# Mix stage of a two-block transformer kernel: three of the four out-projection pieces get their low parts on GpSimd, and the convolution's square is placed ahead of the last copies

## The chip, the cores and the metric

The kernel runs on one core of one Trainium2 chip. The metric is the device time of one execution in microseconds (us). Three timed runs of the kernel before gave 1586.13, 1586.66 and 1586.75 us; the median is 1586.66 us.

## What is computed

The input is 256 tokens of width 1024, in fp32. A first block runs two layers of feed-forward, mixer and feed-forward. A second block, where the change lies, is

```python
hn = rms_norm(h, attn_norm_g[l])
proj = jnp.einsum('bsd,de->bse', hn, w_in[l])
xc, b_gate, c_gate, q, k, v = jnp.split(proj, split_points, axis=-1)
y_conv = short_conv_group(xc, b_gate, c_gate, conv_w[l], conv_out_g[l])
y_attn = diff_attention_group(q, k, v, ...)
mix = jnp.concatenate([y_conv, y_attn], axis=-1)
h = h + jnp.einsum('bse,ed->bsd', mix, w_out[l])
hn2 = rms_norm(h, ffn_norm_g[l]).reshape(Bsz * S, D)
y_ffn = hierarchical_moe(hn2, ...)      # 4 x 8 experts, top 2
```

The first half of `mix` (512 columns) is `b_gate` times a causal convolution of width 3 over `c_gate * xc`, normed in 8 groups; the second half is a four-head differential attention. The 32 experts' weights, 6 MB each, are all read from HBM.

## The kernel before

**Pieces.** Every weight matrix outside the experts goes through a ring of three slots in pieces of 128x2048 fp32. SP's queue loads a piece into `raw`; ACT (ScalarE) rounds it into `high` (`round_piece`, the operation on L249); DVE (VectorE) subtracts, `low = raw - high` (`split_piece`, L253); TensorE multiplies with three products per term (`product`, L258 to L260). The semaphore `split` counts finished subtractions over the whole program, `rounded` the roundings, and `used` the pieces that TensorE is done with. A slot is loaded again (`piece_loads`, L243) when the piece three before it is split, and rounded into when that piece is used.

**The mix stage.** Pieces 0 to 11 are the in-projection, six chunks of 512 columns, each in two pieces; pieces 12 to 15 are the out-projection. Each engine has its own order of work, written out by hand (`mix_pe`, `mix_act`, `mix_dve`, `mix_conv_pool`), and the engines meet at semaphores. The chunks are copied out of PSUM by ACT (`copies(n)`, L1722 for the first 128 tokens and L1725 for the second); `copies(5)` is the value chunk, without which the attention's outputs (`outs`, L1684 to L1687) can't begin. `outs(tt)` waits for the copy of its tokens.

**The convolution.** DVE forms `u` (L1938). GpSimd then issues seven DMAs that write `u`, moved down by one and by two rows, into `shifted` (L1992, L1997). DVE multiplies the unmoved part (`conv_unshifted`, L1886), then splits piece 12, then runs `conv()`: L1891 and L1892 on the moved parts, two sums (L1893, L1894) and the gate (L1897), which raises `m["conv"]`. Each of these reads two tensors in SBUF, as do L1903 and L1911 in `conv_norm()`. ACT squares the result (L1766), DVE sums the squares by group (L1905), ACT takes the root (L1768), DVE inverts it (L1908) and scales (L1911). That raises `h_ready`, for which TensorE waits before it transposes the convolution's half (`turn_half(tt, 0)`, L1673). ACT rounds the transposed half (L1772), DVE subtracts (`low_half`, L1915), and the products of pieces 12 and 13 begin. Pieces 14 and 15 belong to the attention's half and follow.

**Fillers.** `hold_clock(n)` (L1695) issues n products of the identity matrix whose result is not read; in the records each gives two matmuls.

**Behind the stage.** The out-projection is followed by the norm, the router and the expert stage. Its first loads wait on `h_ready`, `split` and `used` (`moe_sp`, L2255 in `load`); from the second batch on, each load waits until TensorE is done with the slot's last contents.

Of the kernel before, what the change touches and what calls it, by code (L numbers as in the profile page):

```python
# [95 lines left out]
def build(nc, t, out):  # L96
    ctx = ExitStack()
    with ctx:
# [65 lines left out]
        def banks(a, n=1):  # L164
            return psum[:, a:a + n, :].rearrange("p b n -> p (b n)")
# [674 lines left out]
        def columns(name, n):  # L840

            c = {"gla_in": (0, 1, 4, 2, 3, 5), "mix_in": (3, 4, 0, 2, 1, 5)}.get(name, range(IN_CHUNKS))[n]
            return slice(c * BANK, (c + 1) * BANK)
# [761 lines left out]
        def both(off, n):  # L1605
            return proj[:, :, off:off + n]
# [9 lines left out]
        def mix_pe(pe):  # L1616
            done = IN_DONE["mix_in"]

            def turn_qk(i):

                pe.wait_ge(m["qk"], i + 1)
                turn_columns(pe, banks(3 + 2 * i, 2), QK + i * D_CONV, DA_HEADS, m["qkT"])

            def dots(hd):

                pe.wait_ge(m["qk_sb"], 2)
                if hd >= 2:
                    pe.wait_ge(m["exp"], hd - 1)
                at = hd * TOKENS
                for c in range(2):  # L1630
                    rows, dst = slice(DA_HD * c, DA_HD * (c + 1)), banks(dot_banks(hd) + c)
                    pe.matmul(dst[:, 0:P], mqT[rows, at:at + P], mkT[rows, at:at + P], start=True, stop=False,
                              skip_group_check=True)
                for c in range(2):
                    rows, dst = slice(DA_HD * c, DA_HD * (c + 1)), banks(dot_banks(hd) + c)
                    ins = pe.matmul(dst[:, P:HEAD], mqT[rows, at + P:at + TOKENS], mkT[rows, at:at + TOKENS],
                                    start=False, stop=True, skip_group_check=True)
                    ins.then_inc(m["dots"], 1)

            def turn_a(hd):  # L1640
                pe.wait_ge(m["a"], hd + 1)
                if hd:
                    pe.wait_ge(m["aT_sb"], hd)
                for j in range(3):
                    ins = pe.transpose(TURN_X[:, j * P:(j + 1) * P], ma[hd % 2][:, j * P:(j + 1) * P], ident[:, :])
                ins.then_inc(m["aT"], 1)

            def after(n, r):
                at = 4 * n + r
                if at == 6:  # L1650
                    turn_qk(0)
                elif at == 10:
                    turn_qk(1)
                elif at == 12:
                    dots(0)
                elif at == 13:
                    dots(1)
                elif at == 15:
                    turn_a(0)
                    dots(2)  # L1660
                elif at == 16:
                    turn_a(1)
                    dots(3)
                elif at == 19:
                    turn_a(2)
                elif at == 20:
                    turn_a(3)

            def turn_half(tt, j):

                dst = banks((ATTN_BANK if j else CONV_BANK)[tt])
                for i in range(4):
                    ins = pe.transpose(dst[:, i * P:(i + 1) * P], h[:, tt, (4 * j + i) * P:(4 * j + i + 1) * P], ident[:, :])  # L1673
                ins.then_inc(turned, 1)

            def outs(tt):
                pe.wait_ge(in_copied[tt], done + IN_CHUNKS)
                pe.wait_ge(m["aT_sb"], DA_HEADS)
                dst = banks(ATTN_BANK[tt])
                for hd in range(DA_HEADS):  # L1680
                    a, col = maT[hd], slice(hd * DA_V, (hd + 1) * DA_V)
                    v0, v1 = (proj[:, i, VV + hd * DA_V:VV + (hd + 1) * DA_V] for i in range(TT))
                    if tt == 0:
                        ins = pe.matmul(dst[:, col], a[:, 0:P], v0, start=hd == 0, stop=True, skip_group_check=True)  # L1684
                    else:
                        pe.matmul(dst[:, col], a[:, P:2 * P], v0, start=hd == 0, stop=False, skip_group_check=True)
                        ins = pe.matmul(dst[:, col], a[:, 2 * P:], v1, start=False, stop=True, skip_group_check=True)  # L1687
                ins.then_inc(m["out"], 1)

            in_quarters(pe, "mix_in", 7, after)  # L1690

            def hold_clock(times):

                for _ in range(times):
                    pe.matmul(banks(3)[:, 0:P], ident[:, :], ident[:, :], start=True, stop=True, skip_group_check=True)  # L1695

            def front(products):
                outs(0)
                outs(1)
                hold_clock(9)  # L1700
                pe.wait_ge(h_ready, H_AT["mix"] + 1)
                for tt in range(TT):
                    turn_half(tt, 0)
                hold_clock(5)
                pe.wait_ge(turn_low, 4 * MIX_TURN + 1)
                products(0, 0)
                pe.wait_ge(turn_low, 4 * MIX_TURN + 2)
                products(0, 1)
                products(1, 0)
                for tt in range(TT):  # L1710
                    pe.wait_ge(h_ready, H_AT["mix"] + 2 + tt)
                    turn_half(tt, 1)
                products(1, 1)
                pe.wait_ge(turn_low, 4 * MIX_TURN + 4)
            out_pe(pe, "mix_out", 8, front)

        def mix_act(act, step):
            b, done = FIRST_PIECE["mix_in"], IN_DONE["mix_in"]

            def copies(n):  # L1720
                act.wait_ge(in_first, done + n + 1)
                act.activation(proj[:, 0, columns("mix_in", n)], banks((2 * n) % 3), ACT.Copy,  # L1722
                               scale=rstd[:, 0:1]).then_inc(in_copied[0], 1)
                act.wait_ge(used, b + 2 * n + 2)
                act.activation(proj[:, 1, columns("mix_in", n)], banks((2 * n + 1) % 3), ACT.Copy,  # L1725
                               scale=rstd[:, 1:2]).then_inc(in_copied[1], 1)

            def qk_root(i):

# [31 lines left out]
            def piece(i):  # L1761
                round_piece(act, b + i)

            def conv_root_act():
                act.wait_ge(m["conv"], 1)
                act.activation(both(XC, D_CONV), both(CG, D_CONV), ACT.Square).then_inc(m["sq"], 1)  # L1766
                act.wait_ge(m["sum"], 3)
                act.activation(conv_root, conv_sum, ACT.Sqrt, scale=8.0 / D_CONV, bias=eps[:, :]).then_inc(m["root"], 1)  # L1768

# [33 lines left out]
            turned_a(2)  # L1803
            turned_a(3)
            piece(13)
            copies(5)
            conv_root_act()
            act.wait_ge(used, b + IN_PIECES)
            for tt in range(TT):
                high_half(tt, 0, tt + 1)  # L1810
# [11 lines left out]
        def mix_dve(dve, step):  # L1822
            b, done = FIRST_PIECE["mix_in"], IN_DONE["mix_in"]

            def piece(i):
                split_piece(dve, b + i)
# [86 lines left out]
            def low_half(tt, j, number):  # L1913
                dve.wait_ge(turn_high, 4 * MIX_TURN + number)
                dve.tensor_tensor(turn_bank(hT_low, tt, j), banks((ATTN_BANK if j else CONV_BANK)[tt]).rearrange(  # L1915
                    "p (k n) -> p k n", n=P), turn_bank(hT_high, tt, j).bitcast(F32), ALU.subtract).then_inc(turn_low, 1)
# [25 lines left out]
            weights(3)  # L1942
            piece(11)
            conv_unshifted()
            piece(12)
            conv()
            conv_norm()
            dve.wait_ge(used, b + IN_PIECES)
            for tt in range(TT):
                low_half(tt, 0, tt + 1)  # L1950
            piece(13)
            for tt in range(TT):
                dve.wait_ge(m["sq"], tt + 4)
                dve.tensor_reduce(out_stat(tt, "sum"),
# [7 lines left out]
                                                   banks(ATTN_BANK[tt])[:, c], out_stat(tt, "inverse")[:, hd:hd + 1], sub_gain,  # L1962
                                                   ALU.mult, ALU.mult)
                ins.then_inc(h_ready, 1)
            piece(14)
            for tt in range(TT):
                low_half(tt, 1, tt + 3)
            out_dve(dve, "mix_out", 8)

        def mix_pool(pool, step):  # L1970
# [14 lines left out]
        def mix_conv_pool(pool, step):  # L1985

            pool.wait_ge(m["u"], 1)
            for rows in (slice(0, EVEN_ROWS), slice(EVEN_ROWS, P)):
                for i in range(2):
                    n = i + 1  # L1990
                    stop = min(rows.stop, P - n)
                    pool.dma_start(by_tile(shifted[i])[rows.start + n:stop + n, :, :],  # L1992
                                   both(XC, D_CONV)[rows.start:stop, :, :]).then_inc(m["shifted"], 16)
            for i in range(2):
                n = i + 1
                for r in range(n):
                    pool.dma_start(shifted[i][r:r + 1, D_CONV:2 * D_CONV],  # L1997
                                   proj[P - n + r:P - n + r + 1, 0, XC:XC + D_CONV]).then_inc(m["shifted"], 16)


        pa = route_tables[:, :]
# [737 lines left out]
```

## Time and profile before

| | us |
|---|---|
| median of the timed runs | 1586.66 |
| profiled execution | 1583.56 |
| its span, first to last instruction | 1581.8 |
| TensorE busy | 1454.2 (92%) |
| VectorE busy | 855.5 (54%) |
| ScalarE busy | 604.5 (38%) |
| GpSimd busy | 33.1 (2%) |

The profile is of one execution; its times are counted from the span's start. The mix stage's in-projection ends at about 1076 us, its out-projection at about 1107 us, and the expert stage fills the rest. Busy shares are averages over stages with different limits, so what follows reads single stages.

### The profile page before, as it was taken

What the parts mean: (1) busy time and instruction counts of PE and PEld (TensorE: products, weight loads), DVE (VectorE), ACT (ScalarE), POOL (GpSimd) and SP (SyncE); (2) the same over time, 40 slices, a digit from 0 to 9 for tenths busy, and PEclk for the clock granted to TensorE, in tenths of its full rate; (3) what the DMA queues carried; (4) which work ended last, traced back from release to release, by engine and by line L of the source; (5) the groups of instructions that cost most, each with busy time, mean ns of one, the idle gap of its engine ahead of it and who ended that gap; (6) DMA issues with size and microseconds to landing.
All of it is one profiled execution on the core that took longest, in us unless ns stands there. A gap on an engine that the chain in (4) does not pass through costs nothing.

```text
span 1581.8 us, 26834 instructions
## 1 busy us (share of the span) xinstructions
PE 1454.2 (92%) x10856; PEld 1139.8 (72%) x10856; DVE 855.5 (54%) x1140; ACT 604.5 (38%) x787; POOL 33.1 (2%) x69
## 2 busy tenths in 40 slices
PE   8999999999999999999999999999977677678677
PEld 7888888888888888877788888778644344345344
DVE  5777688577776777765557776787511101101101
ACT  5443465563445544466554444764200000000001
POOL 4000000000000000000010000010000000000000
PEclk9999999999999999999999999999999889898798
DMA  7565544456464565554356555567699999999995
GB/s 236 199 207 191 188 158 134 133 176 218 165 211 160 187 211 187 177 180 138 117 165 213 186 186 187 178 226 302 279 421 429 430 429 428 430 430 429 430 429 253
DMA packets 149044, 396.68 MB, mean 251 GB/s; under 512 B 8003, under 2 KB 106387, under 8 KB 136704
## 3 DMA queue, kind: packets, MB, share of 16 engines
q1 hardware_dynamic: 147424, 392.20, 66.4%
q0 software_dynamic: 1440, 3.72, 1.0%
q8 instruction: 37, 0.61, 0.2%
q14 instruction: 15, 0.12, 0.0%
q10 hardware_dynamic: 128, 0.03, 0.0%
HBM read 393.83 MB, written 1.05 MB: 250 GB/s over the span
## 4 chain that ended last, share of the span: by engine, by line
PE 77%; DMA 17%; DVE 3%; ACT 1%; issue 1%; SPq 1%; DVEq 0%; POOL 0%; ACTq 0%; POOLq 0%
DMA pair_ring<-in_w_exp_up 17%; PE psum L557 17%; PE psum L258 12%; PE psum L260 12%; PE psum L259 12%; PE psum L563 9%; PE psum L2355 3%; PE psum L2327 2%; PE psum L2380 2%; PE psum L2389 2%; PE psum L1024 1%; DVE low L253 1%; PE psum L2367 1%; PE psum L1435 1%; DVE hT L445 1%
## 5 line engine op out<-in xcount | busy, mean ns | idle before, releaser
L253 DVE TENSOR_TENSOR low<-raw,high 128x2048 fp32r<-128x2048 f32 x179 | 409.3, 2290 | 191.5 <-ACT high L249 190.8
L249 ACT ACTIVATE high<-raw 128x2048 fp32r<-128x2048 f32 x179 | 341.1, 1910 | 123.2 <-PE psum L563 90.2
L557 PE MATMUL psum<-hT,high 128*128 128x512 f32 x1152 | 288.0, 392 | 0.7 <-DVE low L253 0.7
L557 PEld LDWEIGHTS psum<-hT,high 128*128 128x128 f32 x1152 | 209.2, 189 | 39.9 <-DVE low L253 1.0
L2355 PE MATMUL psum<-pair_ring,gain 128*32 128x256 f32 x1536 | 128.9, 509 | 85.2 <-DMA pair_ring<-in_w_exp_up 85.2
L258 PE MATMUL psum<-high,hT 128*128 128x512 f32 x496 | 199.5, 402 | 5.9 <-DVE low L253 3.9
L260 PE MATMUL psum<-high,hT 128*128 128x512 f32 x496 | 193.8, 391 | 0.0
L259 PE MATMUL psum<-low,hT 128*128 128x512 f32 x496 | 193.3, 390 | 0.0
L2355 PEld LDWEIGHTS psum<-pair_ring,gain 128*32 128x32 f32 x1536 | 61.2, 144 | 147.4 <-DMA pair_ring<-in_w_exp_up 90.7
L563 PEld LDWEIGHTS psum<-hT,low 128*128 128x128 f32 x1152 | 157.2, 190 | 11.2
L2494 DVE COPY levels<-psum 128x128 f32<-128x128 f32 x32 | 9.3, 291 | 283.3 <-PE psum L2367 283.3
L563 PE MATMUL psum<-hT,low 128*128 128x256 f32 x1152 | 160.6, 282 | 0.0
L258 PE MATMUL psum<-high,aT_high 128*128 128x512 f32 x352 | 137.9, 392 | 0.2
L259 PE MATMUL psum<-low,aT_high 128*128 128x512 f32 x352 | 137.4, 390 | 0.0
L260 PE MATMUL psum<-high,aT_low 128*128 128x512 f32 x352 | 137.0, 389 | 0.0
L258 PEld LDWEIGHTS psum<-high,hT 128*128 128x128 f32 x496 | 93.2, 188 | 29.0 <-issue 7.0
L704 ACT ACTIVATE inner_sb<-inner_sb 128x256 f32<-128x256 f32 x72 | 30.1, 418 | 219.2 <-DVE inner_sb L774 219.2
L2457 ACT ACTIVATE square<-psum 128x128 f32<-128x128 f32 x32 | 8.9, 277 | 263.9 <-PE psum L2355 263.9
L260 PEld LDWEIGHTS psum<-high,hT 128*128 128x128 f32 x496 | 93.1, 188 | 20.2
L259 PEld LDWEIGHTS psum<-low,hT 128*128 128x128 f32 x496 | 93.3, 188 | 17.7
L260 PEld LDWEIGHTS psum<-high,aT_low 128*128 128x128 f32 x352 | 66.1, 188 | 14.1
L258 PEld LDWEIGHTS psum<-high,aT_high 128*128 128x128 f32 x352 | 66.2, 188 | 13.9 <-DVE aT_low L755 1.2
(358 smaller groups left out, 1465.9 us busy)
## 6 DMA issues: line engine op xcount, KB each, us to landing
pair_ring<-in_w_exp_gate SPq DMA_DIRECT2D x24, 2048.0 KB, 27.1
pair_ring<-in_w_exp_up SPq DMA_DIRECT2D x24, 2048.0 KB, 31.5
raw<-in_ffn_w_gate SPq DMA_DIRECT2D x88, 512.0 KB, 4.0
raw<-in_ffn_w_up SPq DMA_DIRECT2D x88, 512.0 KB, 4.9
raw<-in_ffn_w_down SPq DMA_DIRECT2D x88, 512.0 KB, 4.4
early_pair<-in_w_exp_down SPq DMA_DIRECT2D x16, 2048.0 KB, 24.2
pair_ring<-in_w_exp_down SPq DMA_DIRECT2D x16, 2048.0 KB, 14.3
extra_pairs<-in_w_exp_up SPq DMA_DIRECT2D x8, 2048.0 KB, 21.5
```

The costliest lines, as they stand in the source:

```text
L249: act.activation(high[:, p % RING, :], raw_of(p), ACT.Copy).then_inc(rounded, 1)
L253: dve.tensor_tensor(low[:, p % RING, :], raw_of(p), high[:, p % RING, :].bitcast(F32), ALU.subtract).then_inc(split, 1)
L258: pe.matmul(psum_out, lhs_high, rhs_high, start=start, stop=False, skip_group_check=True)
L259: pe.matmul(psum_out, lhs_high, rhs_low, start=False, stop=False, skip_group_check=True)
L260: return pe.matmul(psum_out, lhs_low, rhs_high, start=False, stop=stop, skip_group_check=True)
L557: pe.matmul(to.rearrange("p (o n) -> p o n", o=2), w_high, both_parts, start=kk == 0, stop=False, skip_group_check=True)
L563: ins = pe.matmul(to[:, 0:TOKENS], w_low, hT_high[:, kk, :], start=False, stop=kk == KD - 1, skip_group_check=True)
L704: act.activation(inner_sb[:, n, 0:TOKENS], inner_sb[:, n, 0:TOKENS], ACT.Silu).then_inc(block_silu, 1)
L2327: ins = pe.matmul(BATCH_X[half][:, k * P:(k + 1) * P], h[:, tt, kk * P:(kk + 1) * P], picks[:, tt * P:(tt + 1) * P], start=tt == 0, stop=t ...
L2355: ins = pe.matmul(out_rows, batch_x[:, kk, j * SLOTS:(j + 1) * SLOTS], w[:, :, kk, c * P:(c + 1) * P], start=kk == 0, stop=kk == KD - 1, s ...
L2380: ins = pe.matmul(ITEM_Y[q * SLOTS:(q + 1) * SLOTS, :], item_aT[:, c * SLOTS:(c + 1) * SLOTS], w[:, c, q * QUARTER:(q + 1) * QUARTER], sta ...
L2389: return pe.matmul(SUM_Y[tt][:, q * QUARTER:(q + 1) * QUARTER], spread[rows, j, tt * P:(tt + 1) * P], item_y[j % 2][rows, :], start=False, ...
```

## The change

GpSimd, after its seven DMAs, waits until `split` shows all pieces up to the in-projection's last, and then runs `split_piece` for pieces 12, 13 and 14. DVE no longer does these three; it waits for them before it splits piece 15. On ACT the convolution's square is moved ahead of `copies(5)`, the group root stands between that chunk's two copies, and `copies(n)` is cut into `copy(n, tt)` for this. On TensorE the filler of 9 ahead of the wait for `h_ready` is dropped, and the one of 5 behind the transposes becomes 3.

```diff
--- before.py
+++ after.py
@@ -1697,11 +1697,10 @@
             def front(products):
                 outs(0)
                 outs(1)
-                hold_clock(9)
                 pe.wait_ge(h_ready, H_AT["mix"] + 1)
                 for tt in range(TT):
                     turn_half(tt, 0)
-                hold_clock(5)
+                hold_clock(3)
                 pe.wait_ge(turn_low, 4 * MIX_TURN + 1)
                 products(0, 0)
                 pe.wait_ge(turn_low, 4 * MIX_TURN + 2)
@@ -1717,13 +1716,17 @@
         def mix_act(act, step):
             b, done = FIRST_PIECE["mix_in"], IN_DONE["mix_in"]
 
+            def copy(n, tt):
+                if tt == 0:
+                    act.wait_ge(in_first, done + n + 1)
+                else:
+                    act.wait_ge(used, b + 2 * n + 2)
+                act.activation(proj[:, tt, columns("mix_in", n)], banks((2 * n + tt) % 3), ACT.Copy,
+                               scale=rstd[:, tt:tt + 1]).then_inc(in_copied[tt], 1)
+
             def copies(n):
-                act.wait_ge(in_first, done + n + 1)
-                act.activation(proj[:, 0, columns("mix_in", n)], banks((2 * n) % 3), ACT.Copy,
-                               scale=rstd[:, 0:1]).then_inc(in_copied[0], 1)
-                act.wait_ge(used, b + 2 * n + 2)
-                act.activation(proj[:, 1, columns("mix_in", n)], banks((2 * n + 1) % 3), ACT.Copy,
-                               scale=rstd[:, 1:2]).then_inc(in_copied[1], 1)
+                for tt in range(TT):
+                    copy(n, tt)
 
             def qk_root(i):
 
@@ -1761,9 +1764,11 @@
             def piece(i):
                 round_piece(act, b + i)
 
-            def conv_root_act():
+            def conv_square_act():
                 act.wait_ge(m["conv"], 1)
                 act.activation(both(XC, D_CONV), both(CG, D_CONV), ACT.Square).then_inc(m["sq"], 1)
+
+            def conv_root_act():
                 act.wait_ge(m["sum"], 3)
                 act.activation(conv_root, conv_sum, ACT.Sqrt, scale=8.0 / D_CONV, bias=eps[:, :]).then_inc(m["root"], 1)
 
@@ -1803,8 +1808,10 @@
             turned_a(2)
             turned_a(3)
             piece(13)
-            copies(5)
+            conv_square_act()
+            copy(5, 0)
             conv_root_act()
+            copy(5, 1)
             act.wait_ge(used, b + IN_PIECES)
             for tt in range(TT):
                 high_half(tt, 0, tt + 1)
@@ -1942,13 +1949,11 @@
             weights(3)
             piece(11)
             conv_unshifted()
-            piece(12)
             conv()
             conv_norm()
             dve.wait_ge(used, b + IN_PIECES)
             for tt in range(TT):
                 low_half(tt, 0, tt + 1)
-            piece(13)
             for tt in range(TT):
                 dve.wait_ge(m["sq"], tt + 4)
                 dve.tensor_reduce(out_stat(tt, "sum"),
@@ -1962,9 +1967,9 @@
                                                    banks(ATTN_BANK[tt])[:, c], out_stat(tt, "inverse")[:, hd:hd + 1], sub_gain,
                                                    ALU.mult, ALU.mult)
                 ins.then_inc(h_ready, 1)
-            piece(14)
             for tt in range(TT):
                 low_half(tt, 1, tt + 3)
+            dve.wait_ge(split, FIRST_PIECE["mix_out"] + 3)
             out_dve(dve, "mix_out", 8)
 
         def mix_pool(pool, step):
@@ -1996,6 +2001,9 @@
                 for r in range(n):
                     pool.dma_start(shifted[i][r:r + 1, D_CONV:2 * D_CONV],
                                    proj[P - n + r:P - n + r + 1, 0, XC:XC + D_CONV]).then_inc(m["shifted"], 16)
+            pool.wait_ge(split, FIRST_PIECE["mix_out"])
+            for p in range(FIRST_PIECE["mix_out"], FIRST_PIECE["mix_out"] + 3):
+                split_piece(pool, p)
 
 
         pa = route_tables[:, :]
```

## Rows read from the trace of the kernel before

**Rows 1.** Busy time by stretch: start:end, length, engines, granted clock, DMA share, GB/s.
```profile
1083.00:1107.00 24.00, 24.00 (x116) 19.90 (x115) 16.55 (x23) 8.49 (x15) 0.00 (x0) 1.00 0.98 405
1130.00:1135.00 5.00, 3.37 (x85) 1.95 (x77) 4.41 (x15) 0.28 (x1) 0.00 (x0) 1.00 0.02 3
1150.00:1155.00 5.00, 4.50 (x93) 2.28 (x81) 1.63 (x3) 0.28 (x1) 0.00 (x0) 1.00 1.01 429
1170.00:1175.00 5.00, 0.42 (x12) 0.15 (x8) 0.00 (x0) 0.00 (x0) 0.00 (x0) 0.99 1.06 452
1175.00:1180.00 5.00, 5.00 (x64) 2.48 (x60) 0.00 (x0) 0.00 (x0) 0.00 (x0) 0.67 1.01 433
```

**Rows 2.** The chain that ended last, 1076 to 1083.5 us: start, us, what.
```profile
1076.15 0.69 ACT proj L1725
1076.84 0.94 ACT proj L1766
1077.80 1.28 ACT L1768
1079.09 0.32 ACT levels L1768
...
1079.72 1.24 DVE h L1911
1081.00 1.09 PE psum L1673 x8
...
1083.21 0.49 PE psum L258
```

**Rows 3.** Timeline of VectorE, 1065 to 1076 us: start, us, instruction, [idle before it].
```profile
1065.50 1.22 DVE L1886 TENSOR_TENSOR proj<-proj,scratch 128x1024 f32<-128x1024 f32 x1
1066.92 2.29 DVE L253 TENSOR_TENSOR low<-raw,high 128x2048 fp32r<-128x2048 f32 x1 [0.20 <-ACT high L249]
1069.13 1.22 DVE L1891 TENSOR_TENSOR scratch<-scratch 128x1024 f32<-128x1024 f32 x1
...
1074.04 1.23 DVE L1897 TENSOR_TENSOR proj<-proj 128x1024 f32<-128x1024 f32 x1
```

**Rows 4.** Timeline of ScalarE, 1065 to 1077 us.
```profile
1064.98 1.91 ACT L249 ACTIVATE high<-raw 128x2048 fp32r<-128x2048 f32 x1
...
1070.77 1.92 ACT L249 ACTIVATE high<-raw 128x2048 fp32r<-128x2048 f32 x1 [2.31 <-PE psum L260]
```

**Rows 5.** Timeline of TensorE, 1076 to 1081 us.
```profile
1075.95 1.05 PE L1684 MATMUL psum<-proj,scratch 128*128 128x128 f32 x8
...
1078.78 2.17 PE L1695 MATMUL psum<-ident 128*128 128x128 f32 x18
```

**Rows 6.** Timeline of all engines, 319.7 to 320.5 us.
```profile
319.77 2.28 DVE L253 TENSOR_TENSOR low<-raw,high 128x2048 fp32r<-128x2048 f32 x1
...
319.92 0.20 POOL L1571 MEMSET scratch<- 128x128 f32 x1 [126.14 <-DVE x L339]
...
320.41 1.79 POOL L2563 TENSOR_SCALAR_AFFINE_SELECT scratch<-scratch 128x128 f32<-128x128 f32 x1
```

**Rows 7.** Timeline of all engines, 27.1 to 27.2 us.
```profile
27.11 2.29 DVE L253 TENSOR_TENSOR low<-raw,high 128x2048 fp32r<-128x2048 f32 x1 [0.69 <-ACT high L249]
27.16 2.46 POOL L2563 TENSOR_SCALAR_AFFINE_SELECT levels<-levels 128x64 f32<-128x64 f32 x1
```

**Rows 8.** GpSimd's instructions by line and shape: busy us, mean ns, idle before.
```profile
L2582 POOL MEMSET levels<- 128x896 f32 x1 | 0.9, 894 | 0.0
...
L2563 POOL TENSOR_SCALAR_AFFINE_SELECT causal<-causal 128x128 f32<-128x128 f32 x1 | 0.3, 301 | 0.1
...
L2583 POOL MEMSET causal<- 128x128 f32 x1 | 0.2, 248 | 0.0
```

**Rows 9.** GpSimd's timeline, 1055 to 1062 us.
```profile
1058.43 1.51 POOL L1997 DMA_DIRECT2D scratch<-proj  x3
```

**Rows 10.** DMA issues, 1055 to 1069 us: KB each, median us to landing.
```profile
scratch<-proj POOLq DMA_DIRECT2D x3, 2.0 KB, 7.4
```

## The prediction

> **What bounds the kernel now.** I read the busy times by stretch first, to see what the mix stage passes on. In the expert stage the DMA engines are the limit: 429 GB/s at a share of 1.01 from 1150 us on, while ahead of it, from 1130 to 1135 us, they move 3 GB/s because the next loads wait for TensorE [rows 1]. The long stream of weights therefore starts when the first batch of experts is through, and that batch starts when the router is, so whatever the mix stage gains or loses moves the stream and the end with it, one for one. From 1083 to 1107 us TensorE is busy for 24.00 of 24 us [rows 1]: once the out-projection has begun, it runs without a gap. So the stage's question is when the first product of piece 12 starts.
>
> The chain that ended last answers it: ACT's last copy (1076.15), the convolution's square (1076.84), the table load for the root (1077.80, 1.28 us) and the root (1079.09), DVE's scaling (1079.72), the transposes (1081.00), the first product at 1083.21 [rows 2]. TensorE had finished `outs` by 1078.78 and ran fillers for 2.17 us while it waited [rows 5]. Of the 2.2 us from transposes to first product, ACT's rounding and DVE's subtraction of the transposed half are a latency that stays. Hence at most 1081.00 - 1078.78 = 2.2 us can be won, whatever becomes earlier in front.
>
> **The change part by part.**
>
> *Piece 12 leaves DVE.* `conv_unshifted` ends at 1066.72 and L1891 starts at 1069.13 [rows 3]: 2.41 us go out of the convolution's path. The moved rows don't bind: the last of the three small DMAs is issued at about 1059.45 and lands some 7.4 us later, at 1066.85 [rows 9, 10]. With nothing else, L1897 would end 2.3 us earlier than its 1075.27.
>
> *GpSimd's subtractions.* How long one takes, no row shows. A memset, which only writes, takes 248 ns for 128 columns and 894 for 896, so 0.84 ns per column over 140 ns fixed; 2048 columns in one pass make 1.86 us. The select, which reads and writes, takes 301 ns for 128 columns: 53 ns above the memset, half of the 108 ns of a second pass [rows 8]. Two reads and half a pass for the write give 0.14 + 2.5 x 1.72 = 4.4 us, two reads and a whole write 5.3 us. The bounds are 1.86 and 5.3; I take 4.4, the value nearest to the select, the only row that reads.
>
> *What stands beside them.* GpSimd can start piece 12 when ACT has rounded it, at 1066.89, and piece 13 at 1072.69 [rows 4]. That is in the middle of the convolution, where DVE runs six instructions of 1.2 us back to back, each with two inputs in SBUF. The trace shows what happens when these two engines meet. A select that GpSimd starts at 320.41, 0.64 us into a subtraction on DVE, takes 1.79 us where its like takes 0.30, and ends 0.15 us after the subtraction, which runs from 319.77 to 322.05; the memset at 319.92, inside the same subtraction, takes its usual 0.20 [rows 6, 8]. At 27.16 it happens again: 2.46 us, to an end 0.22 us after DVE's [rows 7]. So an instruction of GpSimd that reads SBUF is held for as long as a two-input instruction of DVE lasts, and one that only writes is not. No row has GpSimd first and DVE second, as GpSimd's reading instructions before are too short. The bounds are that DVE isn't held at all, and that it is held for GpSimd's whole 4.4 us. I take the second, the mirror of what rows 6 and 7 show.
>
> The Trainium skill says the same of the side that no row shows: by SBUF — State Buffer, § Who interferes with whom, DVE's second input and GpSimd's reads go through one port pair, which is an exclusive lock, and who issues first keeps it for its whole instruction. By it the change would be a loss, as in the sum below.
>
> *The sum.* GpSimd starts piece 12 at 1066.95 and ends at 1071.35. L1891 and L1892 run behind it, to 1073.71 (1.22 and 1.14 us at their spacing). Piece 13, waiting since 1072.69, takes the port there, to 1078.11. L1893, L1894 and L1897 need 3.75 us and end at 1081.86, 6.6 us later than now (in general 2T - 2.2 for a subtraction of T).
>
> *The square ahead of the copies.* ACT now holds the value chunk's first copy behind the square, so behind `m["conv"]`. From 1081.86: square 0.98, copy 0.65, table load 1.28, root 0.32, so 1085.09; DVE's scaling ends 1.55 us later, at 1086.64 [rows 2]. In the old order the square would wait for both copies; this order saves 0.7 us if the convolution is early. As it is late, `outs` pays: the first copy ends at 1083.5 where TensorE wanted it at 1075.95, the second, behind the root, at about 1085.75. `outs` for the second tokens takes 1.89 us (1076.89 to 1078.78) [rows 5], so TensorE transposes at 1087.7, not 1081.00, and begins the products 2.2 us later, at 1089.9: 6.7 us late at full clock (2T - 2.1 in general).
>
> *The clock.* TensorE then idles from 1076.15 to 1083.5. After an idle stretch (0.42 us busy in 1170 to 1175) the granted clock averages 0.67 over 1175 to 1180 [rows 1], that is, 3.3 of 5 us at 1.2 instead of 2.4 GHz. If it falls here, about 1 us of the second `outs` runs at half speed: 0.5 us. Bounds: 0, and 3.0 if `outs` and the transposes (1.89 and 1.09 us) all run so.
>
> *Fillers.* The 18 matmuls of 2.17 us [rows 5] stood in a wait, so leaving them out costs or saves nothing by itself; if the wait is longer than before, they are missed as cover for the clock, which is in the bound above. The second filler, 10 matmuls before and 6 now at 0.12 us each, stays under the 2.2 us of latency: 0.
>
> *Other queues.* On SP's queue the load of piece 15 waits for piece 12's subtraction, 1071.35 instead of 1069.21; it is not rounded before the attention's half is transposed, 8 us into the products, so this is free. Behind it stand the expert loads that wait for `h_ready`; they move with the stage. On DVE, piece 15 now waits for piece 14 on GpSimd. Piece 14 is rounded some 6 us after the first product, done 4.4 us later, and wanted at 12 us: 1.6 us spare. Piece 15's own subtraction ends no later against the products than now. In the attention's part DVE reads PSUM beside one SBUF tensor, so I price contention there at 0.
>
> Together 6.7 + 0.5 = 7.2 us. On the profiled execution (1583.56 us: span 1581.8 and 1.76 around it) that gives 1590.8; the median of the runs is 3.1 us above that execution, and the same difference on it gives 1593.9.
>
> **The rivals.**
>
> *The port costs DVE nothing.* Either DVE isn't held, or it keeps the port through its run. Then L1897 ends at 1073.0, scaling at about 1077.9, and `outs` at 1078.78 is the bound: -2.2 us, 1584.5. In the second form GpSimd gets in at 1074.1, ends at 1078.5 and holds only L1911, to about 1079.7: -1.3 us, 1585.4. This is the case on the other side; it decides if DVE's L1891 after 1066.95 keeps its 1.22 us. For it: only GpSimd was seen waiting [rows 6, 7]. Against: DVE's instructions wait for one another at semaphores, with the port free between them, and in both rows GpSimd ended 0.2 us behind DVE.
>
> *One subtraction in the convolution, the second behind it.* L1897 ends at 1077.5 (+2.2); piece 13 then holds the port from 1078.7 to 1083.1, and L1911, due at 1081, ends at 1084.3: the first product at 1086.5, +3.3 us, 1590.0. For it: DVE's gaps are 0.03 us. Against: the one pause suffices.
>
> *GpSimd is far slower than its rows,* 10 us for one subtraction: 2T - 2.1 = 18 us, 1604.6. Nothing speaks for it but that no subtraction on GpSimd stands in the trace.
>
> *More than 2.2 us is won,* by a part that I don't see: 1583.0 or less.
>
> **How the numbers follow.** Two subtractions in the convolution 0.58, one 0.12, none 0.25, slow GpSimd 0.03, a larger gain 0.02. The likeliest one's own range runs from T = 2.8 without the clock (+3.5) to T = 5.3 with 2 us of it (+10.5): 1590.2 to 1597.2. With the other cases the range is 1584.2 to 1597.2; what is left out is the slow GpSimd, the larger gain, and the tails of the rest. About 0.2%, 3.2 us, is what a measurement of this kernel can tell from no change. Slower by more: 0.54 of the 0.58, 0.07 of the 0.12 and the 0.03, 0.64. Within: 0.04, 0.05 and 0.22 of the 0.25, 0.31. Faster: 0.05.
>
> **What would show it.** Right: L1891 or L1893 takes 3 to 6 us in the profile, L253 stands on GpSimd with 4 to 5 us each, the second one inside the convolution; `outs` waits for ACT's copies until about 1083, the first product comes near 1090, and from 1150 us on everything stands some 7 us later. Wrong: the convolution's instructions all keep 1.22 us and the products begin at 1081 (the port is free), or L1893 to L1897 run undisturbed and L1911 is long (one subtraction). A TensorE gap inside the products, ahead of piece 13, 14 or 15, would show a wait that I priced at nothing.

## The result and the profile after

| | before | after |
|---|---|---|
| median of the timed runs, us | 1586.75 | 1595.80 |
| profiled execution, us | 1583.56 | 1595.05 |
| VectorE busy, us | 855.5 | 858.5 |
| GpSimd busy, us | 33.1 | 48.2 |

The ratio is 1.0056 [1.0044, 1.0068]: 9.05 us slower, with an interval of 7.0 to 10.8 us. Forecast were 1593.9 us (+7.2) and a range of 1584.2 to 1597.2.

Line numbers have moved: L1891 to L1897 of `conv()` are now L1898 to L1904, ACT's square, root and copies L1769, L1773 and L1724, the down product L2388 (was L2380); the rows of each kernel below carry that kernel's own numbers. In the profiled execution of after, ACT rounds piece 12 at 1067.82 us, not at 1064.98 [rows 4]. These 2.84 us come from ahead of the change and differ from execution to execution (0 to 4 us in the ones below; "after, filled" is the same program up to there and has none). "In the stage" means a time with the kernel's own offset of this kind taken off.

GpSimd's timeline, 1065 to 1104 us of after (start, us, instruction, [idle before it]):

```profile
1069.88 5.38 POOL L253 TENSOR_TENSOR low<-raw,high 128x2048 fp32r<-128x2048 f32 x1 [7.09 <-ACT high L249]
1075.61 5.16 POOL L253 TENSOR_TENSOR low<-raw,high 128x2048 fp32r<-128x2048 f32 x1 [0.35 <-ACT high L249]
1098.53 4.59 POOL L253 TENSOR_TENSOR low<-raw,high 128x2048 fp32r<-128x2048 f32 x1 [17.77 <-ACT high L249]
```

VectorE's, the same columns; it answers to [rows 3]:

```profile
1069.55 1.23 DVE L1898 TENSOR_TENSOR scratch<-scratch 128x1024 f32<-128x1024 f32 x1
1070.69 5.65 DVE L1899 TENSOR_TENSOR scratch<-scratch 128x1024 f32<-128x1024 f32 x1
1076.38 5.47 DVE L1900 TENSOR_TENSOR proj<-proj,scratch 128x1024 f32<-128x1024 f32 x1
...
1083.14 1.23 DVE L1904 TENSOR_TENSOR proj<-proj 128x1024 f32<-128x1024 f32 x1
```

The two engines take turns. GpSimd's first subtraction is issued at 1069.88 inside L1898 and gets going when that ends, at 1070.78; from there it takes 4.48 us, to 1075.26. L1899 stands for all of that and ends 1.08 us later. GpSimd's second, issued at 1075.61, waits for that end and ends at 1080.77; L1900 stands behind it and ends at 1081.85. The third one meets nothing: 4.59 us.

ScalarE's timeline, then TensorE's (the former answers to the ACT rows of [rows 2], the latter to [rows 5]):

```profile
1084.40 1.06 ACT L1769 ACTIVATE proj<-proj 128x1024 f32<-128x1024 f32 x1 [8.87 <-DVE proj L1904]
1085.37 0.67 ACT L1724 ACTIVATE proj<-psum,rstd 128x512 f32<-128x512 f32 x1
1086.05 1.28 ACT L1773 ACT_TABLE_LOAD   x1
...
1087.56 0.67 ACT L1724 ACTIVATE proj<-psum,rstd 128x512 f32<-128x512 f32 x1
```

```profile
1086.09 2.08 PE L1684 MATMUL psum<-proj,scratch 128*128 128x128 f32 x8 [7.14 <-ACT proj L1724]
...
1088.28 0.79 PE L1686 MATMUL psum<-proj,scratch 128*128 128x128 f32 x2
...
1090.74 1.04 PE L1673 MATMUL psum<-ident,h 128*128 128x128 f32 x8
...
1092.89 0.50 PE L258 MATMUL psum<-high,hT 128*128 128x512 f32 x1 [0.44 <-DVE hT L1922]
```

TensorE waits 7.14 us for the first copy. The first product stands at 1092.89, in the stage at 1090.05, against 1083.21 [rows 2]: 6.84 us late. TensorE's rows by stretch (columns as in [rows 1]) show the clock in this wait, the products, and the first batch of experts:

```profile
1083.00:1089.00 6.00, 2.79 (x11) 2.50 (x12) 4.97 (x6) 3.80 (x5) 0.00 (x0) 0.50 0.01 3
...
1093.00:1113.00 20.00, 20.00 (x93) 16.58 (x94) 9.19 (x18) 7.03 (x11) 4.59 (x1) 1.00 1.00 422
...
1144.00:1148.00 4.00, 3.60 (x34) 1.60 (x34) 0.53 (x3) 0.07 (x1) 0.00 (x0) 0.57 0.00 0
```

The products run without a gap, as before. The last row has what nobody forecast: the first batch's down product at a granted clock of 0.57. Its row in TensorE's timeline, of after and then of before:

```profile
1144.40 3.46 PE L2388 MATMUL psum<-early_pair,levels 128*32 128x256 f32 x32 [1.85 <-DVE levels L2502]
```

```profile
1134.50 1.93 PE L2380 MATMUL psum<-early_pair,levels 128*32 128x256 f32 x32 [1.64 <-DVE levels L2494]
```

The two profiled executions differ by 11.49 us: 2.84 ahead of the change, 6.84 in the stage, 1.53 in this product, and 0.3 elsewhere, 0.2 of it in the wait in front of this product (1.85 for 1.64).

### The profile page after: what moved, and what is told of

It is laid out like the page before. It is cut to its first block, busy times and chain, and to the rows that moved or that the text cites. A ratio compares the mean times of both kernels' runs of the same rounds, so it can differ in the third digit from the quotient of the medians.

```text
span 1593.3 us, 26792 instructions
## 1 busy us (share of the span) xinstructions
PE 1458.2 (92%) x10834; PEld 1139.2 (72%) x10834; DVE 858.5 (54%) x1137; ACT 604.6 (38%) x787; POOL 48.2 (3%) x72
## 4 chain that ended last, share of the span: by engine, by line
PE 75%; DMA 17%; DVE 5%; ACT 2%; issue 1%; SPq 1%; DVEq 0%; POOL 0%; ACTq 0%; POOLq 0%
DMA pair_ring<-in_w_exp_up 17%; PE psum L557 17%; PE psum L258 12%; PE psum L259 11%; PE psum L260 11%; PE psum L563 9%; PE psum L2363 3%; PE psum L2388 2%; PE psum L2335 2%; PE psum L2397 2%; DVE low L253 1%; PE psum L1024 1%; PE psum L2375 1%; PE psum L1435 1%; DVE hT L445 1%
## 5 line engine op out<-in xcount | busy, mean ns | idle before, releaser
L253 DVE TENSOR_TENSOR low<-raw,high 128x2048 fp32r<-128x2048 f32 x176 | 402.7, 2291 | 193.3 <-ACT high L249 192.9
## 6 DMA issues: line engine op xcount, KB each, us to landing
pair_ring<-in_w_exp_gate SPq DMA_DIRECT2D x24, 2048.0 KB, 27.1
```

Of the source, the lines that this page charges most:

```text
L253: dve.tensor_tensor(low[:, p % RING, :], raw_of(p), high[:, p % RING, :].bitcast(F32), ALU.subtract).then_inc(split, 1)
```

## The experiments

All were timed in five rounds, beside runs of the kernel before on the same chip (its medians: 1585.9 to 1586.6 us).

| kernel | median, us | against before | ratio |
|---|---|---|---|
| no GpSimd | 1588.13 | +2.1 | 1.0015 [1.0006, 1.0024] |
| GpSimd only | 1593.57 | +7.5 | 1.0047 [1.0033, 1.0061] |
| piece 12 behind the norm | 1584.62 | -1.4 | 0.9997 [0.9988, 1.0006] |
| the same, GpSimd late | 1586.07 | 0.0 | 1.0001 [0.9992, 1.0010] |
| one subtraction in the convolution | 1590.25 | +3.7 | 1.0026 [1.0017, 1.0035] |
| writes on GpSimd | 1586.55 | 0.0 | 1.0000 [0.9991, 1.0008] |
| reads on GpSimd | 1589.09 | +2.5 | 1.0018 [1.0009, 1.0028] |
| piece 12 behind the norm, filled | 1582.95 | -3.6 | 0.9981 [0.9972, 0.9989] |
| before, filled | 1586.59 | +0.5 | 1.0001 [0.9990, 1.0011] |
| after, filled | 1592.79 | +6.7 | 1.0043 [1.0030, 1.0057] |
| fillers only | 1586.60 | +0.7 | 1.0000 [0.9991, 1.0010] |
| order only | 1591.19 | +5.3 | 1.0035 [1.0023, 1.0047] |

**No GpSimd:** the change with the three subtractions back on VectorE, at their old places.

```diff
             conv_unshifted()
+            piece(12)
             conv()
...
+            piece(13)
...
+            piece(14)
...
-            pool.wait_ge(split, FIRST_PIECE["mix_out"])
-            for p in range(FIRST_PIECE["mix_out"], FIRST_PIECE["mix_out"] + 3):
-                split_piece(pool, p)
```

> The change without GpSimd: DVE subtracts pieces 12, 13 and 14 at the places of the kernel before; ACT's order and the fillers are those of the change. Theory (an instruction of GpSimd that reads SBUF holds DVE's two-input instructions for its whole length, and that is nearly all of the loss): L1904 ends where it did before, the convolution's first product comes within 0.5 us of before, the time is 1586 to 1588 us. Rival (the square ahead of the copies, or the missing fillers, are the loss): 1593 to 1597 us.

The convolution ran undisturbed and ended, in the stage, where it did before, so some 7 of the change's 9 us come with GpSimd's subtractions. But the kernel was 2.1 us slower, just above what I had expected: `outs` waited 0.85 and 1.04 us for the copies and its second half ran at half clock, which made the first product 1.6 us late in the stage, not within 0.5. In the profiled execution, the slowest of its eleven, the router's fillers (3.91 us) and the down product (3.33) lost more to the clock.

**GpSimd only:** `piece(12)` to `piece(14)` moved to GpSimd, ACT's order and the fillers as before.

> GpSimd subtracts pieces 12, 13 and 14 as in the change; ACT's order and the fillers are those of the kernel before. Theory: the convolution ends 6.6 us late as in the change, but outs no longer waits for the copies, so the first product is 5.0 us late: 1591 to 1593.5 us, less than the change by some 2 us. Rival (ACT's order is the loss): no slower than 1587 us, as the convolution is then early. Rival (DVE is slowed in proportion to GpSimd's traffic, not held): all six instructions of the convolution are longer by about the same, none takes over 3 us.

Timeline of GpSimd and VectorE:

```profile
1069.91 4.61 POOL L253 TENSOR_TENSOR low<-raw,high 128x2048 fp32r<-128x2048 f32 x1 [7.09 <-ACT high L249]
1070.12 5.48 DVE L1891 TENSOR_TENSOR scratch<-scratch 128x1024 f32<-128x1024 f32 x1 [0.53 <-DMA scratch<-proj]
1075.53 1.21 DVE L1892 TENSOR_TENSOR scratch<-scratch 128x1024 f32<-128x1024 f32 x1
1075.64 5.52 POOL L253 TENSOR_TENSOR low<-raw,high 128x2048 fp32r<-128x2048 f32 x1 [1.11 <-ACT high L249]
1076.77 5.47 DVE L1893 TENSOR_TENSOR proj<-proj,scratch 128x1024 f32<-128x1024 f32 x1
```

Here GpSimd came first with the port free: it takes its 4.61 us and L1891, issued 0.21 us later, stands until then. The first product is 6.9 us late in the stage, as in the change, and not 5.0 as expected: behind a wait of 5.28 us the transposes took 1.97 us, not 1.09, and the fillers behind them were slow too.

**Piece 12 behind the norm,** no GpSimd: `piece(12)` stands on VectorE behind `conv_norm()`; order and fillers as in the change.

> No GpSimd; DVE subtracts piece 12 behind L1918, the convolution's last step, instead of ahead of the convolution, and 13 and 14 where it did before; ACT's order and fillers of the change. Theory: this is the gain that the change could have had with a free port; the convolution ends 2.3 us earlier, outs is the bound, the first product comes 2.2 us earlier: 1584 to 1585 us. Rival (piece 12 is then late for the first product): 1586.5 to 1588 us, with TensorE waiting for L253.

TensorE's timeline:

```profile
1081.06 0.50 PE L258 MATMUL psum<-high,hT 128*128 128x512 f32 x1 [0.43 <-DVE hT L1922]
```

The first product came 2.25 us early in the stage: the gain that the first rival would have had, if the port cost nothing. In the profiled execution that gain was used up again, as the router's fillers took 1.34 us longer (3.62 for 2.28) and the down product 3.00 us for 1.93; the median is 1.4 us below before, which is not apart from zero.

**GpSimd late:** this kernel, with pieces 13 and 14 on GpSimd behind VectorE's piece 12.

> As e2_behind_norm, but GpSimd subtracts pieces 13 and 14, and only once DVE has subtracted piece 12, so behind the convolution, where DVE's instructions read one tensor in SBUF and one in PSUM. Theory: no DVE instruction is longer than before, GpSimd takes 4.5 us each, nothing waits for it: 1584 to 1585 us, as e2_behind_norm. Rival (GpSimd's work slows DVE whatever DVE reads, or comes late for TensorE): 1588 us or more, with long instructions on DVE or a gap of TensorE ahead of piece 13.

Timeline of GpSimd and VectorE:

```profile
1081.46 4.60 POOL L253 TENSOR_TENSOR low<-raw,high 128x2048 fp32r<-128x2048 f32 x1 [20.62 <-DVE low L253]
1081.54 1.29 DVE L1922 TENSOR_TENSOR hT<-psum,hT 128x512 fp32r<-128x512 f32 x2 [0.16 <-ACT hT L1777]
```

`low_half`, with one input in PSUM and one in SBUF, keeps its 1.29 us inside GpSimd's run. Off the convolution, GpSimd's help costs VectorE nothing that shows. A gain can't be seen either: the median is that of before, above the 1584 to 1585 us expected, with the first product 1.8 us early in the stage, the router's fillers at 3.70 us and the down product at 3.45.

**Writes and reads.** To the kernel with piece 12 behind the norm, GpSimd work on an idle tensor was added in the convolution: five memsets, or two subtractions of half a piece's width. Nothing reads the result; SP's first expert load was made to wait for it, in both.

```diff
+            pool.wait_ge(rounded, FIRST_PIECE["mix_out"] + 1)
...
+            for i in range(2):
+                step(pool.tensor_tensor(spare, gain[:, 1, :], gain[:, 1, :], ALU.subtract))
```

> e2_behind_norm with five more memsets of 1024 columns on GpSimd into a tensor that is free in this stage, from the end of piece 12's rounding on, 4.7 us in all: GpSimd writes in SBUF and reads nothing. Theory (the reading side of the port is what DVE loses): the convolution's six instructions keep 1.2 us each and the time is that of e2_behind_norm, 1584 to 1586 us. Rival (any work of GpSimd in SBUF holds DVE): L1898 and others are longer, 1588 to 1590 us.

> As e6_writes, but in place of the memsets two subtractions of 1024 columns with two inputs in SBUF, 2.3 us each, into the same free tensor. Theory: two of the convolution's instructions are held for up to 2.3 us each, the convolution ends some 4.6 us later than in e2_behind_norm, the first product some 4.5 us: 1588 to 1590 us. Rival (what the change lost is that its subtractions' results came late, not the port): as e2_behind_norm, 1584 to 1586 us, since nothing uses these results.

Timeline with the memsets, then with the subtractions:

```profile
1070.72 5.01 POOL L2009 MEMSET inner_sb<- 128x1024 f32 x5 [6.99 <-ACT high L249]
1071.40 1.23 DVE L1898 TENSOR_TENSOR scratch<-scratch 128x1024 f32<-128x1024 f32 x1 [0.89 <-DMA scratch<-proj]
1072.54 1.22 DVE L1899 TENSOR_TENSOR scratch<-scratch 128x1024 f32<-128x1024 f32 x1
```

```profile
1068.39 4.73 POOL L2009 TENSOR_TENSOR inner_sb<-gain 128x1024 f32<-128x1024 f32 x2 [7.00 <-ACT high L249]
1068.56 2.81 DVE L1898 TENSOR_TENSOR scratch<-scratch 128x1024 f32<-128x1024 f32 x1 [0.40 <-DMA scratch<-proj]
1071.29 2.91 DVE L1899 TENSOR_TENSOR scratch<-scratch 128x1024 f32<-128x1024 f32 x1
1074.23 1.23 DVE L1900 TENSOR_TENSOR proj<-proj,scratch 128x1024 f32<-128x1024 f32 x1
```

Five microseconds of writing hold nothing. Of the two reading subtractions, which one row shows together, the first takes 1.89 us and the second 2.76, in which it waits for L1898's end. They lengthen L1898 by 1.6 us and L1899 by 1.7, so the convolution ends, in the stage, 3.6 us later than without them (4.6 were expected, at 2.3 us each; 0.3 is a later start) and the first product stands 5.0 us later. Nothing waits for their result but the first expert load, as with the memsets, so a late piece is excluded as the cause; what remains is the reading itself.

The median with the memsets is 0.0, above the 1584 to 1586 us expected, though no instruction is long: the convolution waited 0.89 us for the moved rows, so the first product is only 1.5 us early in the stage, and the router's fillers took 3.90 us, the down product 3.57.

**One subtraction in the convolution:** the change, with GpSimd waiting for the convolution's `h_ready` ahead of piece 13.

> The change, but GpSimd waits for the convolution's h_ready ahead of piece 13, so that one subtraction and not two falls among the convolution's instructions. Theory (T per subtraction, T = 4.4 us): the first product comes 4.4 us earlier than in the change, 2 to 2.5 us later than before, 1588 to 1591 us. Rival (one meeting costs as much as two): 1594 us or more.

VectorE's timeline, then TensorE's:

```profile
1069.16 5.65 DVE L1899 TENSOR_TENSOR scratch<-scratch 128x1024 f32<-128x1024 f32 x1
1074.85 1.22 DVE L1900 TENSOR_TENSOR proj<-proj,scratch 128x1024 f32<-128x1024 f32 x1
```

```profile
1088.68 0.50 PE L258 MATMUL psum<-high,hT 128*128 128x512 f32 x1
```

Only L1899 is long: one meeting holds VectorE for 4.4 us where two hold it for 8.7. The median is as expected, the first product is not: it is 4.4 us late in the stage, not 2 to 2.5, and of that the second `outs` at half clock (3.58 for 1.89) and slower transposes make 2.1.

**Fillers only, order only.** The kernel before with either of the change's other parts.

> The kernel before with the change's fillers alone (the one of 9 dropped, the one of 5 now 3). Theory A, in which the fillers' place matters for the clock behind them: the transposes after 2.2 us of idle TensorE, the router's fillers or the first batch's down product run at half clock, and the median rises by 1 to 3 us, to 1587.5 to 1589.5. Rival B, in which the ACT order is what cost the version without GpSimd its 2 us: no change, 1585.5 to 1587, and the down product keeps 1.93 us.

> The kernel before with the change's order on ACT alone (square ahead of the last copies), fillers of 9 and 5 kept. With the convolution ending at 1075.3 as before, the first copy comes some 1 us late and the second some 2.3 us, so that the second outs ends with the scaling, near 1081.1: the first product +0.1 to +0.5 at full clock, up to +1.5 if outs falls to half clock. Theory A: nothing falls behind the stage, the filler of 9 stands in front of the transposes and now costs up to its 2.17 us, because TensorE comes to it late: 1586.5 to 1589. Rival B: the down product falls to half clock by the order alone, another +1.5.

TensorE's timeline with the change's fillers, then with its order on ACT:

```profile
1084.48 1.09 PE L1673 MATMUL psum<-ident,h 128*128 128x128 f32 x8 [2.06 <-DVE h L1910]
...
1086.68 0.50 PE L258 MATMUL psum<-high,hT 128*128 128x512 f32 x1 [0.43 <-DVE hT L1914]
```

```profile
1081.02 1.16 PE L1684 MATMUL psum<-proj,scratch 128*128 128x128 f32 x8 [0.87 <-ACT proj L1725]
1083.22 0.49 PE L1686 MATMUL psum<-proj,scratch 128*128 128x128 f32 x2 [1.03 <-ACT proj L1725]
...
1083.93 0.64 PE L1686 MATMUL psum<-proj,scratch 128*128 128x128 f32 x2
...
1086.49 2.42 PE L1695 MATMUL psum<-ident 128*128 128x128 f32 x18
1088.74 1.04 PE L1673 MATMUL psum<-ident,h 128*128 128x128 f32 x8
```

The fillers cost nothing: with its offset of 3.47 us taken off, the first product stands at 1083.21, that of before to the hundredth. The order is not free: the second copy comes 2.3 us late, the second `outs` then takes 3.27 us for 1.89, most of it at half clock, and the filler of 9 stands in front of the transposes. The first product is 3.64 us late in the stage; the median says more (2.2 us above what I expected at most; its interval reaches down to 3.6), and what the rest would be I did not find. The profiled execution, its offset taken off, is 4.1 us longer than that of before.

**Filled.** Fillers were put where TensorE waits behind the stage: three ahead of the router's `h_ready`, six ahead of the first batch's down product.

```diff
                 turn_inner(0, b)
+                if b == 0:
+                    for _ in range(6):
+                        pe.matmul(banks(1)[:, 2 * P:3 * P], ident[:, :], ident[:, :], ...)
                 down(0, b)
...
+            hold_clock(pe, 3)
             pe.wait_ge(h_ready, H_AT["n8"] + TT)
```

> e2_behind_norm with fillers at two waits behind the mix stage: 3 (6 matmuls) ahead of the wait for the last rows of h in the router, 6 (6 matmuls) ahead of the first batch's first down product. In e2_behind_norm's profile the granted clock was 0.50 there twice. Theory (the 2.2 us won by placing piece 12 behind the convolution are partly given back by the clock): it stays at 1.00 there, 1582.5 to 1584.5 us. Rival (the clock's falls are a matter of the single run and the fillers don't reach them): 1584 to 1586 us, as e2_behind_norm.

> The kernel before, with the added fillers of the filled version alone (three ahead of the router's wait, six ahead of the first batch's first down product). Theory A, in which the filled version owes its 3.6 us to the earlier first product (2.2 us) and to a clock that is kept behind the stage: in the profile before the router and that down product already ran at full clock, so in runs like the profiled one the fillers give nothing, over all runs they give 0 to 1.5 us; 1585.1 to 1586.6. Rival B, in which the fillers alone are the gain: 1583 or less, within 1 us of the filled version.

> The changed kernel with the same added fillers. If the part of its loss that the prediction did not foresee is the half clock in the first batch's down product, that product takes 1.93 us again instead of 3.46, and the median falls by 1.5 to 2 us to 1593.8 to 1594.5, that is, 7 to 8 us above the kernel before, which leaves the predicted +7.2. Rival: the fillers do nothing or the clock falls elsewhere for it, and the median stays at 1595.3 or more.

TensorE's busy time by stretch in the kernel with piece 12 behind the norm, without and then with these fillers:

```profile
1117.00:1120.00 3.00, 3.00 (x17) 3.00 (x16) 2.72 (x15) 0.00 (x0) 0.00 (x0) 0.51 1.00 423
1133.00:1137.00 4.00, 3.56 (x35) 1.85 (x36) 0.58 (x3) 0.38 (x1) 0.00 (x0) 0.64 0.00 0
```

```profile
1117.00:1120.00 3.00, 2.50 (x21) 2.30 (x20) 2.79 (x15) 0.21 (x2) 0.00 (x0) 1.00 1.03 434
1133.00:1137.00 4.00, 3.89 (x57) 2.45 (x60) 1.01 (x3) 0.38 (x1) 0.00 (x0) 1.00 0.30 61
```

With the clock kept, the early convolution's gain arrives: the profiled execution is 2.05 us shorter than that of before, offsets taken off, and by its median this version beats both kernels, 3.6 us below before (interval 1.7 to 4.4). Its interval and that of the version without the fillers, timed on another chip, still touch, so what the fillers add rests on the two profiles. On the kernel before the same fillers give nothing. On the change they bring the down product back to 1.93 us; the median falls to +6.7, by more than the product's 1.5 us, though its interval (4.8 to 9.0 us) overlaps the change's:

```profile
1143.22 1.93 PE L2388 MATMUL psum<-early_pair,levels 128*32 128x256 f32 x32 [0.31 <-DVE levels L2507]
```

## Why the prediction was right

*Who bounds the stage, and one for one.* Right: +6.84 us at the first product, +9.68 at the out-projection's end where the offset of 2.84 is included, so nothing was lost or won between.

*GpSimd's duration.* Taken 4.4, measured 4.43 to 4.61 us: the select, the only row that read [rows 8], was the right neighbour. The Trainium skill's GPSIMD Engine Reference, § Performance versus the Vector engine, has 4497 ns for an fp32 `tensor_tensor` add of 2048 columns; the undisturbed 4.59 us agrees. The prediction's own working hit this size partly by luck: for 1024 columns it gives 2.3 us, and the first of the two reading subtractions above, which nothing held up, took 1.89 (both its inputs are one tensor).

*The mirror of rows 6 and 7.* Right: GpSimd holds VectorE as VectorE had held GpSimd. The writes and the reads show that it is the reading, and the kernel with one subtraction that the cost goes by the meeting. This is the lock of the Trainium skill's SBUF — State Buffer, § Who interferes with whom, and the trace agrees on its other side too: L1891, issued 0.21 us behind GpSimd, took 5.48 us. The order of the turns was another than in the sum, which had GpSimd first and two of VectorE's instructions between its two: VectorE came first, 0.24 us ahead of the sum's start, and one instruction stood between. The convolution ended 6.26 us late against 6.6 forecast, by that earlier start and because a held instruction ends 1.08 us behind GpSimd's, not 1.22.

*The rivals.* That VectorE keeps the port through its run failed at the first hand-over: GpSimd, issued at 1069.88 inside L1898, was next, although L1899 was issued at 1070.69, ahead of L1898's end and with no semaphore between the two. The pause at a semaphore, which the prediction held against this rival, was not needed there. One subtraction alone came about only when GpSimd was made to wait, and then cost +3.7.

*ACT's order.* The ends of the two copies and of VectorE's scaling were forecast at 1083.5, 1085.75 and 1086.64; in the stage they are 1083.20, 1085.39 and 1086.36. That the order costs where the convolution is not early is shown by "order only". That it pays where it is early is not shown: no run has the early convolution with the old order.

*The clock.* Inside the sum 0.5 us, measured 0.57 (the second `outs` took 2.46 us, not 1.89). The bound of 3.0 was needed: in the profiled execution of the filled change the first product is 8.5 us late in the stage, 1.7 more, with the whole second `outs` at half clock.

*Fillers, queues, piece 14.* All at 0, and all 0: TensorE's only wait in the products is the 0.44 us in front of them. That the moved rows don't bind held in the profiled execution of the change; in seven of the nine profiled kernels that take piece 12 out of the convolution's way, the convolution waited 0.20 to 0.89 us for them.

*What was missing* is the first batch's down product, 1.5 us at half clock. I followed the clock to the transposes and priced everything behind them one for one. Together with it, 7.2 would have been 8.7, beside the 9.05 measured; the interval holds both.

*Left open:* why the clock falls there. That product ran wholly or partly at half clock (2.74 to 3.57 us) in all seven profiled kernels that have both the change's order on ACT and its fillers, without the added ones; it kept 1.93 us in the four with at most one of the two (before, GpSimd only, fillers only, order only). The wait ahead of it doesn't tell them apart: 1.64 us in before and in the kernel with piece 12 behind the norm, with 1.93 and 3.00 us behind it. One profile each is not enough to call this a cause.

## What to carry to other kernels

Before work is handed to GpSimd, look at what VectorE does at that moment, not at how idle GpSimd is: if GpSimd's instruction reads SBUF and VectorE's has two inputs there, each meeting can cost VectorE the whole length of GpSimd's (4.2 to 4.4 us of 4.5 here). Look also for the reorder that needs no other engine: moving the same subtraction 11 us down VectorE's own order brought the first product 2.25 us forward. And follow the clock behind the stage that was changed: here a stage that ended 2 us earlier brought that much to the end of the profiled execution only once the next waits were covered.

## What the runs showed of the hardware

- When both engines want the port, it changes hands at each instruction's end, and in these timelines the one issued first is next: one of VectorE's (1.2 us) between two of GpSimd's (4.5 us).
- TensorE's clock can stay at its upper level through an idle stretch of 2.06 us ("fillers only": granted 1.00, transposes 1.09 us behind it) and fall in another kernel after waits of 0.87 and 1.03 us ("order only": granted 0.57 over 1083 to 1087 us, 0.64 us for what takes 0.39).
